# The opening of a macaron encoder layer: conditioning a quarter ahead, norm work in front of the tiles, and another order of weight loads

## The reference

```python
mod = jax.nn.silu(c) @ w_ada + b_ada                  # (B, 9D)
sh1, sc1, gt1, sh2, sc2, gt2, sh3, sc3, gt3 = jnp.split(mod, N_MOD, axis=-1)
h = modulate(rmsnorm(x, g_ffn1), sh1, sc1)            # h * (1 + scale) + shift
x = x + 0.5 * gt1[:, None, :] * swiglu(h, w_ffn1_in, w_ffn1_out)
...                                                   # mixer with sh2, sc2, gt2; second SwiGLU with sh3, sc3, gt3
```

## Time and profile before

| | |
|---|---|
| three runs | 1958.72, 1982.29, 2092.65 us; median 1982.29 |
| profiled execution | 1960.46 us |
| its span on the slowest core, core 3 | 1958.9 us (cores: 1936.3 to 1958.9) |
| mean granted TensorE clock, core by core | 0.972 to 0.983 |
| TensorE matmul busy | 1822.9 us, 93% of the span |
| VectorE, ScalarE, GpSimd busy | 760.4, 768.5, 134.6 us |

### The profile page before, as it was taken

How to read it: one execution, slowest core, us unless ns; L and a number is a source line. 1 busy time by engine, 2 the same in 40 slices (tenths; PEclk the granted TensorE clock), 3 DMA queues, 4 the chain that set the end, 5 groups by cost and what they waited for, 6 DMA issues and landing times.

```text
span 1958.9 us, 35558 instructions; the slowest of 8 cores (1936.3 to 1958.9 us)
## 1 busy us (share of the span) xinstructions
PE 1822.9 (93%) x13360; PEld 966.5 (49%) x13360; DVE 760.4 (39%) x1401; ACT 768.5 (39%) x1496; POOL 134.6 (7%) x221
## 2 busy tenths in 40 slices
PE   3798899999998499999999999999899999999997
PEld 1244445554444256556565656565344444544443
DVE  1233123222356155554554555544562123322245
ACT  2454100111255366566556565566572110011132
POOL 2012100110003300000000000000000000000000
PEclk9899899999999799999999999999999999999998
DMA  9601910886225232223231323211622210322112
GB/s 173 187 4 18 160 25 2 139 136 97 65 98 118 56 66 70 58 57 77 48 79 35 80 36 93 52 47 33 206 44 43 33 31 8 65 44 33 17 64 119
DMA packets 42262, 137.91 MB, mean 70 GB/s; under 512 B 5456, under 2 KB 7856, under 8 KB 38992
## 3 DMA queue, kind: packets, MB, share of 16 engines
q0 software_dynamic: 25328, 80.99, 25.5%
q1 hardware_dynamic: 16768, 54.65, 7.9%
HBM read 180.18 MB, written 36.22 MB: 110 GB/s over the span
## 4 chain that ended last, share of the span: by engine, by line
PE 84%; DMA 5%; DVE 4%; ACT 3%; issue 3%; POOL 1%; DVEq 0%; ACTq 0%; SPq 0%; POOLq 0%
PE pb L460 80%; PE pb L458 3%; DMA wsall<-w1i 2%; DVE tw L632 1%; DMA RX<-xs 1%; ACT H L470 1%; DMA fd<-RX 1%; ACT tw L470 1%; DVE RX L683 1%; PE pb L1242 1%; DMA kT<-RX 0%; ACT RG L470 0%; DVE RX L644 0%; ACT L470 0%; DVE RG L669 0%
## 5 line engine op out<-in xcount | busy, mean ns | idle before, releaser
L460 PE MATMUL pb<-H,wsall 128*128 128x512 bf16 (+1 forms) x5760 | 1166.2, 351 | 48.4 <-ACT H L470 24.3
L460 PEld LDWEIGHTS pb<-H,wsall 128*128 128x128 bf16 x5760 | 512.6, 98 | 554.7 <-issue 86.7
L470 ACT ACTIVATE tw<-pb 128x512 bf16<-128x512 f32 (+3 forms) x320 | 169.5, 532 | 677.1 <-PE pb L460 667.7
L470 ACT ACTIVATE RG<-pb 128x512 bf16<-128x512 f32 (+3 forms) x688 | 344.5, 532 | 183.5 <-PE pb L460 157.6
L460 PE MATMUL pb<-RG,wsall 128*128 128x512 bf16 (+1 forms) x2080 | 389.0, 349 | 9.0 <-DVE RX L683 8.7
L669 DVE TENSOR_TENSOR RG<-pb,tw 128x512 bf16<-128x512 f32 (+1 forms) x218 | 132.9, 611 | 503.5 <-PE pb L460 448.3
L460 PEld LDWEIGHTS pb<-RG,wsall 128*128 128x128 bf16 x2080 | 186.9, 98 | 208.7 <-issue 14.3
L460 PE MATMUL pb<-RX 68*128 68x512 bf16 (+3 forms) x640 | 215.3, 349 | 26.9 <-ACT RX L470 26.9
L458 PEld LDWEIGHTS pb<-RX,RG 128*128 128x128 bf16 x2176 | 139.2, 97 | 108.0 <-issue 6.9
L683 DVE SCALAR_TENSOR_TENSOR RX<-pb,DER,RX 128x512 f32<-128x512 f32 (+1 forms) x192 | 112.4, 594 | 187.5 <-PE pb L460 182.1
L458 PE MATMUL pb<-RX,RG 128*128 128x65 bf16 x2176 | 169.7, 193 | 3.1 <-ACT RG L470 2.6
(11 more groups left out here) (97 smaller groups left out, 702.4 us busy)
## 6 DMA issues: line engine op xcount, KB each, us to landing
wsall<-w_in POOLq DMA_DIRECT2D x32, 512.0 KB, 6.5
wsall<-w_ada POOLq DMA_DIRECT2D x28, 512.0 KB, 13.5
wsall<-w1i POOLq DMA_DIRECT2D x22, 512.0 KB, 19.1
wsall<-w2i POOLq DMA_DIRECT2D x22, 512.0 KB, 8.2
RX<-xT SPq DMA_DIRECT2D x4, 2048.0 KB
xs<-RX SPq DMA_DIRECT2D x4, 2048.0 KB
kT<-RX SPq DMA_DIRECT2D x32, 256.0 KB
vo<-RX SPq DMA_DIRECT2D x32, 256.0 KB
```

The costliest lines, as they stand in the source:

```text
L460: ins = e.matmul(o, lhsT=l, rhs=r, start=st, stop=sp)
L470: return P.op("scalar", lambda e: e.activation(out=out, in_=in_, func=func, **kw), reads=reads, writes=writes)
```

## The change

In the opening, ada_slice(q + 1) is issued ahead of the tile quarter q, so TensorE has the conditioning matmuls of the next quarter in its order before the tile matmuls of this one. The DMA order follows: w1i 0 and w1i 1 are both issued behind the loads of quarter 1.

In the walk over blocks, the norm steps of PRE stand in front of tile j, no longer behind it, and the statistics stand behind tile 3 in block 0 and behind tile 1 in blocks 1 to 3 (before: behind tile 4 and tile 2). In blocks 1 to 3 the modulations are dealt out as 3, 3, 2 in front of tiles 3, 4, 5 (before: 2, 3, 3 behind tiles 3, 4, 5).

In the ring, w1i 8 is loaded ahead of the four tiles of kind 2, kind 2 is computed behind strip 8 (before 7), kind 3 behind strip 12 (before 8), and kinds 4 to 8 one strip later each. w1i 10 gets slot 6, which is free at the release of the first seven strips. The slots of everything behind are renamed to fit, also in the later stages, where the order of the loads is the same.

```diff
         for j in range(8):
             plan_j("w1i", w1i, j, j)
+        plan_j("w1i", w1i, 8, 4)
         plan_ada(2, [0, 1, 2, 3])
-        plan_j("w1i", w1i, 8, 4)
         plan_j("w1i", w1i, 9, 5)
-        plan_ada(3, [6, 7, 0, 1])
-        plan_j("w1i", w1i, 10, 2)
-        plan_wo("w1o", w1o, 0, [3, 4, 6, 7, 0, 1])
+        plan_j("w1i", w1i, 10, 6)
+        plan_wo("w1o", w1o, 0, [7, 0, 1, 2, 3, 4])
         plan_j("w1i", w1i, 11, 5)
-        plan_j("w1i", w1i, 12, 2)
-        plan_ada(4, [3, 4, 6, 7])
-        plan_j("w1i", w1i, 13, 0)
-        plan_ada(5, [1, 5, 2, 3])
+        plan_j("w1i", w1i, 12, 6)
+        plan_ada(3, [7, 0, 1, 2])
+        plan_j("w1i", w1i, 13, 3)
+        plan_ada(4, [4, 5, 7, 0])
+        plan_j("w1i", w1i, 14, 1)
+        plan_ada(5, [2, 6, 3, 4])
...
-            if q < 2:
-                ring.pump(q + 1)
+            if q == 1:
+                ring.pump(2)
...
-        for q in range(4):
-            ada_slice(q)
+        def mods_of(q):
             for k in (2 * q, 2 * q + 1):
                 n_mod(0, k, 0, 0)
-            if q == 3:
-                alias_seed([b for l_ in GB[0:8] for b in l_], [v_[1] for v_ in ada_early.values()])
+
+        ada_slice(0)
+        mods_of(0)
+        for q in range(1, 4):
+            ada_slice(q)
             next(first)
+            mods_of(q)
+        alias_seed([b for l_ in GB[0:8] for b in l_], [v_[1] for v_ in ada_early.values()])
+        next(first)
...
-        PRE = [[[], [], many("sq", 0, 4), many("sq", 4, 8), [("stats", 0)] + many("mod", 0, 2), many("mod", 2, 5),
-                many("mod", 5, 8)],
-               [many("sq", 0, 4), many("sq", 4, 8), [("stats", 0)], many("mod", 0, 2), many("mod", 2, 5),
-                many("mod", 5, 8), []]]
+        PRE = [[[], [], many("sq", 0, 4), many("sq", 4, 8), many("mod", 0, 2), many("mod", 2, 5), many("mod", 5, 8)],
+               [many("sq", 0, 4), many("sq", 4, 8), [], many("mod", 0, 3), many("mod", 3, 6), many("mod", 6, 8), []]]
         for tb in range(5):
             for j in range(JB1):
-                if tb > 0 or j > 1:
-                    ffn_in("w1i", j, tb)
                 if tb < 4:
                     for what, k in PRE[tb > 0][j]:
                         if what == "sq":
                             n_sq(tb + 1, k)
-                        elif what == "stats":
-                            n_stats(tb + 1)
                         else:
                             n_mod(tb + 1, k, 0, 0)
+                if tb > 0 or j > 1:
+                    ffn_in("w1i", j, tb)
+                if tb < 4 and j == (3, 1)[tb > 0]:
+                    n_stats(tb + 1)
...
-        ADA_AT = {7: 2, 8: 3, 12: 4, 13: 5, 14: 6, 15: 7, 16: 8}
+        ADA_AT = {8: 2, 12: 3, 13: 4, 14: 5, 15: 6, 16: 7, 17: 8}
```

More of the change, by code:

```diff
@@ L416, in build_program @@
             plan_j("w1i", w1i, j, j)
+        plan_j("w1i", w1i, 8, 4)
         plan_ada(2, [0, 1, 2, 3])
-        plan_j("w1i", w1i, 8, 4)
         plan_j("w1i", w1i, 9, 5)
-        plan_ada(3, [6, 7, 0, 1])
-        plan_j("w1i", w1i, 10, 2)
-        plan_wo("w1o", w1o, 0, [3, 4, 6, 7, 0, 1])
+        plan_j("w1i", w1i, 10, 6)
+        plan_wo("w1o", w1o, 0, [7, 0, 1, 2, 3, 4])
         plan_j("w1i", w1i, 11, 5)
-        plan_j("w1i", w1i, 12, 2)
-        plan_ada(4, [3, 4, 6, 7])
-        plan_j("w1i", w1i, 13, 0)
-        plan_ada(5, [1, 5, 2, 3])
-        plan_j("w1i", w1i, 14, 4)
-        plan_ada(6, [6, 7, 0, 1])
-        plan_j("w1i", w1i, 15, 5)
[L431 to L434, removed]
+        plan_j("w1i", w1i, 12, 6)
[4 more added lines that the diff above has]
+        plan_ada(5, [2, 6, 3, 4])
+        plan_j("w1i", w1i, 15, 5)
+        plan_ada(6, [7, 0, 1, 2])
+        plan_j("w1i", w1i, 16, 6)
+        plan_ada(7, [3, 4, 5, 7])
+        plan_j("w1i", w1i, 17, 0)
+        plan_ada(8, [1, 2, 6, 3])
+        for j_, s_ in ((18, 4), (19, 5), (20, 7), (21, 2)):
             plan_j("w1i", w1i, j_, s_)
-        plan_wo("w1o", w1o, 1, [0, 1, 6, 3, 5, 2])
-        aslots = [7, 4, 6, 3, 5, 2]
+        plan_wo("w1o", w1o, 1, [0, 1, 3, 6, 4, 5])
+        aslots = [7, 2, 3, 6, 4, 5]
         for c in range(8):
@@ L441, in build_program @@
         for q in range(4):
-            ring.add(("wout", q), [6, 3, 5, 2][q],
+            ring.add(("wout", q), [3, 6, 4, 5][q],
                      w_out[q * 256:(q + 1) * 256, :].rearrange("(j p) n -> p j n", p=128), 2048)
-        cyc = [7, 4, 0, 1, 6, 3, 5, 2]
+        cyc = [7, 2, 0, 1, 3, 6, 4, 5]
         nxt = 0
```

## The result

The changed kernel takes 1933.63 us (median of 4 runs, 1932.67 to 1956.15) beside 1970.51 us for the kernel before (4 runs, 1958.28 to 2092.65). The ratio is 0.9889, with a 95% interval from 0.9844 to 0.9934: 1.1% less, which is under the 2% from which the prediction calls a kernel faster. The ratio is not the quotient of the two medians, since runs that a slowed die made longer stay out of it; where the text says *undisturbed* it means the runs without a pair of cores at a granted clock of 0.81 (shown with the first experiment), which are some 25 us shorter, and the intervals take in both. The profiled execution took 1932.67 us, with a span of 1931.0 us on core 5, the slowest of cores at 1922.3 to 1931.0 us. Measured again (the first experiment) the ratio is 0.9899 [0.9829, 0.997].

A forecast was written before the change was run, and what follows sets the result against it. TensorE, busy for 93% of the span, was taken to lose time in waits and half-clock stretches. Gains of 3.6 + 3.45 + 11.2 + 8.2 = 26.5 us from 1960.46 gave 1934 us, range 1918 to 1960.

The forecast's parts named there:

- The sum: Gains in the opening, block 0, blocks 1 to 3 and the ring added together: 26.5 us less.
- Opening: Block 0's first tile quarters: reordered loads and conditioning cover waits for H; gain 3.6 us, bounds 1.5 to 6.3.
- rival B: Clock rises within the opening, tiles behind it start at full clock; gain 32 to 35 us, 1927; chance 0.10.
- Nothing waits before tile 4: Block 0: x lands at 60, squares finish before tile 4, due 67.0; no cost, up to 2.4 us if late.
- rival A: Squares of block 1 block ScalarE, or opening loads slip; gain about 19 us, 1941; chance 0.14.
- Block 0: Statistics behind tile 3 instead of 4 start the chain to the next block sooner; gain 3.45 us.
- Blocks 1 to 3: Statistics behind tile 1 instead of 2 cover the end-of-block waits for H; gain 11.2 us, 9 if cover is short.
- ring: Around strip 8: w1i 8 loaded first, conditioning a strip later, removing load waits; gain 8.2 us, at least 5.2.
- C: Ring starves in strips 12 to 17, weights landing with the whole burst; 30 us net lost, 1990; chance 0.04.
- D: Time won up to 340 us is waited for again at attention's entry; no gain, 1960; chance 0.10.

The follow-up runs named there:

- the first experiment: The changed kernel with no edit, timed again beside its three parts alone; ratio 0.9899 [0.9829, 0.997] against the kernel before.
- The opening alone: The kernel before with only the opening's new order of conditioning and loads, ring and norm steps as before; 1952.41 us, ratio 0.9965.
- norm steps with ring: The kernel before with the norm steps' and the ring's parts of the change, without the opening's; 1936.94 us, ratio 0.9868.
- The sooner x: Changed kernel with block 0's modulations as 5 and 3 before tiles 4 and 5, x block 1 released by the ninth load, not tenth; 1926.57 us, ratio 0.985.
- the part alone: The kernel before with only the ring's new load order and later strips for kinds 2 to 8; 1952.62 us, ratio 0.9941.
- the norm steps alone: The kernel before with only the norm steps and statistics moved, opening and ring as before; 1970.02 us, ratio 1.0051.
- w1i 0 as third load: The changed kernel with w1i 0 loaded ahead of quarter 1's loads again; 1953.91 us in one execution.
- the modulations early: The changed kernel with block 0's modulations as 5 and 3 in front of tiles 4 and 5, none before tile 6; 1929.63 us, ratio 0.9856.

## Why the prediction held, step by step

**The total.** 1933.63 us against 1934. By the landmarks the gain is 27.4 us at the output phase; kind 3's 1.6 us is paid after it, and 25.4 is there at attention's first matmul and 24.5 in the mean span (1951.2 to 1926.6). The sum said 26.5.

**Opening, 3.6 us, bounds 1.5 to 6.3: mis-sized.** The eighth load came at 39.20 and the tenth at 44.86, where 39.3 and 45.5 were taken. But the last quarter ended at 50.8, not at 53.4: the clock rose near 48 us, which the prediction had as the first half of rival B and as its upper bound. The opening alone is worth 7.7 us of TensorE's time on core 1 (5.1 in the quarters, 2.6 in tiles 2 to 4 at full clock) and 6.8 at the statistics in the mean.

**"Nothing waits before tile 4": wrong.** The landing was taken as 60 and was 60.05, and the squares ended where that puts them. The step that failed is when TensorE would ask: tile 3 ends at 60.0, not at 65, so the statistics wait 4.94 us. What the clock gave, the wait took back, and the statistics began at 64.94, about where the sum put them (tile 4 due at 67.0, less 1.7 for the statistics: 65.3). Two misses cancelled; that the forecast held here is partly luck. The squares' place on ScalarE costs nothing that can be told (putting them back behind the tiles changed 0.2 us, in one execution): of rival A its data is right, its queue is not. The Trainium skill (TensorE: Matmul & The Clock Gate, Architectural detail) has ScalarE's queue strictly first in, first out; the rows agree, since the Silu at 62.14 stands behind the squares that waited, yet nothing needed it sooner.

This is also why the parts don't add: alone, opening 7.35 and norm steps with ring 24.6 make 31.95 at the output phase, and together they give 27.4. Both bring the statistics of block 1 forward, and neither can bring them ahead of x and 4.7 us of squares: at the statistics 6.8 and 4.5 us would make 11.3, and together they give 7.5, which is 3.8 of the 4.6 us that are missing. The sooner x moves this bound itself and brings 2.7 us at the output phase; the modulations shorten the chain behind it, 2.4 us.

**Block 0, 3.45 us.** From the end of the statistics (68.31) to block 1 (84.30) are 15.99 us, 15.94 before; the gap is 4.94 (about 5.3 forecast), and two tiles behind it take 9.72 us where 7.07 would do, the 2.7 left in place. Block 1 starts 6.65 us sooner in the mean; 3.6 + 3.45 = 7.05 was forecast.

**Blocks 1 to 3, 11.2 us; ring, 8.2.** From block 1 to strip 9 core 3 took 228.60 - 90.03 = 138.57 us before and core 5 takes 201.45 - 84.30 = 117.15 after: 21.4, where 11.2 + 8.2 + the 1.6 of kind 3 make 21.0. No wait for H stands at the ends of blocks 1 to 3, and none for weights near strip 8. That the ring's part brings its gain by itself is shown by the part alone; that w1i 8's place is what brings it is argued, from the two waits that went. The load time of 3.2 us in the forecast is 3.5 by the two releases that it names; w1i 8 would then be there sooner still, so nothing hangs on it.

**Rivals C and D fell.** From 300 to 640 us the list of TensorE's waits on core 5 has no transfer in it, and 380 to 400 is still 20.00 busy:

```profile
PE pb L461 <- ACT RX L471: 8.5, 5, 3.5
...
PE pb L461 <- ACT scr L471: 1.4, 2, 1.1
...
PE pb L461 <- DVE RX L684: 0.4, 1, 0.4
```

The standstill at the entry of attention moved forward with the work; its first matmul comes 25.4 us sooner, so little was waited for again.

## What to carry to other kernels

When a stretch is tightened, ask again when each datum behind it is first needed: a load that is in time for an engine at half clock isn't when the clock rises, and the cure is then the load's release, not the order on the engine that reads it. Parts that pull the same landmark forward don't add beyond its next bound, so measure them together as well as alone. And a part can lose alone what it saves in company, here to a lowered clock that goes when another part removes the wait ahead of it; look at the granted clock core by core before blaming the edit.

## What was not expected of the hardware

**A granted clock of 0.81 on pairs of cores.** Beside 0.50 and 1.00 (1.2 and 2.4 GHz) stretches of some 160 to 170 us stand at 0.81 (200 to 360 on core 3 of the norm steps alone, 74 to 235 on core 7 of the first experiment, 53 to 225 on core 4 with w1i 0 as third load; short pieces at half clock behind waits lie within the last two). In the kept traces they are always on both cores of a pair (0 and 1, 2 and 3, 4 and 5, 6 and 7) and cost some 24 to 30 us of a core's time. In those three traces each begins some 6 to 10 us behind a restart of TensorE at half clock, twice after some 4 us at 1.00. By spans and mean clocks all 12 runs of the norm steps alone had one, and five of the six with the ring added had none. But a restart isn't enough: cores 4 and 5 of the norm steps alone restart behind the same wait and stay at 1.00, and by their spans most runs of the kernel before do too. Which restarts lead to 0.81 is open; nothing was tried beyond taking the wait away. The Trainium skill (TensorE: Matmul & The Clock Gate, Part 1) tells of a limit at 13/16 of the clock, 0.8125, for a whole die once a third core on it runs dense matmuls, held as long as the load lasts. The level agrees; the rest doesn't: single pairs show it while the other cores of their die stand at 1.00, it ends with the load going on (1.00 at 260 us on core 7 above), and mostly eight dense cores run at 1.00.

**A load in two halves finished later than whole.** On core 0 the second half of x block 1 was there at 62.5, the whole at 60.3, both issued at about 45 while weight loads filled the transfers (DMA share 1.0). In the means of the cores the whole took 14.5 us from its issue, and the halves 11.2 and 17.5; with the modulations early it is the same, 14.5 against 11.3 and 17.6. One load sooner in the order brought the whole in 3.2 us sooner and quarter 3's conditioning 0.2 us later.
